# Two attentions of a float32 encoder trunk: other orders in their first stretches and around the start of their output projections

## The chip, the cores and the metric

One Trainium2 chip, one of its cores. The metric is device time in microseconds (us) of one launch of the whole program; lower is better. Engines: PE is TensorE, ACT ScalarE, DVE VectorE, POOL GpSimd, SP SyncE (it issues most DMAs). Each runs its own instruction stream in order and waits on semaphores.

## The reference, cut to what matters

Two layers over x of 1024 tokens by 1024 features, float32:

```python
for i in range(DEPTH):                    # DEPTH = 2
    hn = rmsnorm(x, norm_mix[i])
    if i == 0:  x = x + windowed_gqa_attention(hn, w_qkv, w_o, sink)    # 16 heads of 64, 4 KV groups, |t-s| <= 128
    else:       x = x + differential_attention(hn, w_qkv, w_o, lam, subln_g, lambda_init)   # 8 heads, two maps each
    x = x + hierarchical_moe(rmsnorm(x, norm_ffn[i]), ...)              # 32 experts, top-1 group, top-2 experts
return rmsnorm(x, final_norm)
```

Both attentions project `hn @ w_qkv`, form softmax(q k^T + bias) v by blocks of 128 queries, and multiply the heads' outputs by `w_o`. In the second, each head's output also goes through an RMSNorm of its own before `w_o`.

## The kernel before, in words

The program is a row of blocks: attention 0 (`windowed_attention`), routing and experts of layer 0, attention 1 (`differential_attention`), routing and experts of layer 1, final norm. All engines meet at the end of each. Every large product is made in three float32r passes: each operand is split into a high part (a cast on ScalarE) and a low part (a subtraction on VectorE or GpSimd), and `three_passes` (lines 365 to 367) multiplies hi by hi, lo by hi and hi by lo. One slice k of a product is a contraction over 128.

**First stretch of an attention.** `Norm` walks over the 8 token tiles (128 tokens each). For tile tt ScalarE squares and sums (line 302) and takes the root (305), VectorE makes the normalised rows (335), TensorE turns them in 8 transposes (358) into two PSUM banks, ScalarE copies them out as the high part (314) and VectorE subtracts (276) to get the low part. Both loops run the copy and the subtraction of tile tt - 2 in step tt. In steps 5, 6 and 7 ("meanwhile") ScalarE and VectorE also split three column blocks j of the first head's weights (407, 413). In attention 0 x comes by four DMAs of two tiles each; in attention 1 two gathered expert rows per tile are added to x first (line 234, twice per tile). TensorE turns tiles 0 to 5, then does projection piece 0 (24 matmuls of 512 columns), turns tiles 6 and 7, then does pieces 1 to 5. A piece (j, n) needs all low parts of tile half n and those of weight block j.

**Attention blocks.** Attention 0 goes over 4 groups, attention 1 over 8 heads, each with 8 query blocks i: scores on TensorE, bias and maximum on VectorE (698; 1413), exponentials on ScalarE, normalising or mixing on VectorE (713; 1430), turns on TensorE (814; 1548), copies on ScalarE (608; 1359), the product with v on TensorE. The groups and heads but the last run in a loop, and the last is written out apart.

**Output projection.** `OutProjection` reads `w_o` by 8 row blocks k through three staging buffers (SyncE loads block k + 3 once k's low part is done). In the last group or head ScalarE casts block i in query block i (474) and GpSimd subtracts (478). After all query blocks, tile tt of the heads' outputs is split (650 and 674; in attention 1 first scaled, 1486, and turned, 1597, then 1377 and 1493), TensorE multiplies it with all 8 weight blocks (48 matmuls, 6 per k), and VectorE adds x and clears the banks (501). In attention 1 the roots of all 8 tiles' sums (1371) are taken after the last head.

Of the kernel before, what the change touches and what calls it, by code (L numbers as in the profile page):

```python
# [21 lines left out]
P = 128  # L22
T = 1024
D = 1024
NT = T // P
# [159 lines left out]
class Loaded(Resident):  # L185


    def __init__(self, t, x_rows):
        self.t, self.x_rows = t, x_rows
        self.loaded = [t.sem(f"x_loaded_{i}") for i in range(NT // 2)]  # L190

    def load(self, sp):
        for i, loaded in enumerate(self.loaded):
            sp.dma_start(self.t.x[:, 2 * i:2 * i + 2, :], self.x_rows[2 * i * P:2 * (i + 1) * P, :]
                         .rearrange("(a p) n -> p a n", p=P)).then_inc(loaded, 16)

    def complete(self, eng, tt):
        eng.wait_ge(self.loaded[tt // 2], 16)
# [43 lines left out]
class Norm:  # L242
# [3 lines left out]
    def __init__(self, t, name, number, sb, banks, source, tiles_T=0, rows_dram=None, bufs=2):  # L246
# [47 lines left out]

    def scalar(self, act, meanwhile=()):

        for tt in range(NT + 2):
# [9 lines left out]
            if 0 <= tt - NT // 2 - 1 < len(meanwhile):  # L307
                meanwhile[tt - NT // 2 - 1]()
            if tt >= 2:
                done = tt - 2  # L310
# [3 lines left out]
                act.copy(self.tile_T(done) if self.tiles_T else self.hi[:, :, done * P:(done + 1) * P],  # L314
                         self.turned_tile(done)).then_inc(self.copied, 1)

    def vector(self, dve, meanwhile=(), second=None):
# [3 lines left out]
        for tt in range(NT):  # L321
# [22 lines left out]
            if not self.tiles_T and tt >= 2:  # L344
                self.low_part(dve, tt - 2)
            if 0 < tt - NT // 2 <= len(meanwhile):
                meanwhile[tt - NT // 2 - 1]()
        if not self.tiles_T:
            self.low_part(dve, NT - 2)
            self.low_part(dve, NT - 1)  # L350
# [19 lines left out]
class Projections:  # L370
# [45 lines left out]
    def tensor(self, pe, out, step, o, first, ks=range(KD)):  # L416


        j, n = self.order[o]
        if first and o == 0:  # L420
            for tt in range(NT - 2):
                self.norm.turn(pe, tt)
        if first and o == 1:
# [14 lines left out]
class OutProjection:  # L438
# [42 lines left out]
    def tensor(self, pe, tt):  # L481
        pe.wait_ge(self.o_lo_done, 2 * tt + 2)
        for k in range(KD):
# [10 lines left out]
        last.then_inc(self.done, 1)  # L494
# [10 lines left out]
def windowed_attention(t, gain, w_qkv, w_o, sink, x_rows, args):  # L505
# [10 lines left out]
    with ExitStack() as ctx:  # L516
# [44 lines left out]
        with nc.Block() as block:  # L561
            @block.sync
            def _(sp):
                t.gain.load(sp, gain)
                norm.source.load(sp)
                sp.dma_start(sinks[:, :], sink.broadcast_to((P, NQ))).then_inc(sink_loaded, 16)

                projections.load(sp, 0)
# [20 lines left out]
            def _(act):  # L589
# [1512 lines left out]
```

## Time and profile before

| | us |
|---|---|
| median of 3 runs (range) | 2495.68 (2493.53 to 2496.23) |
| the profiled execution's own time | 2497.94 |
| its span | 2496.3 |
| TensorE busy, share of span | 2307.5, 92% |
| VectorE busy | 1870.3, 75% |
| ScalarE busy | 1554.3, 62% |
| GpSimd busy | 264.7, 11% |
| attention 0 / attention 1, from the span's start | about 2 to 443 / 1074 to 1820 |

The profile page gives the span in 40 slices; in the slices of the two attentions TensorE is at 9 tenths except at their starts, and in the expert stages DMA is at 9 tenths. Busy shares are averages over the stages. An instruction's idle time stands in square brackets with what released it; matmul ends are modelled, and start to start is the better measure.

### The profile page before, as it was taken

Reading aid. Unit: us, or ns where it says so; the run is one execution under the profiler, and the core shown is the slowest. Engines: PE = TensorE matmul, PEld = TensorE weight load, DVE = VectorE, ACT = ScalarE, POOL = GpSimd, SP = SyncE. Lnnn points to the kernel's source line nnn. Section 1 sums busy time; section 2 is a strip of 40 time slices with the busy share of each in tenths; the row PEclk is TensorE's granted clock in tenths of the full one; section 3 lists DMA queues with packets and bytes.
Section 4 is the critical chain, followed back from the end, with each engine's and each line's share of the span. In section 5 each row is a group of like instructions: output and inputs, shape, how many; then the busy total and the mean of one; then the engine's idle time right before and its main releaser. Section 6 shows DMA issues by size and latency. Waiting matters only on the chain. (4 is left out here: it accounts for less than half of the span.)

```text
span 2496.3 us, 34756 instructions
## 1 busy us (share of the span) xinstructions
PE 2307.5 (92%) x11480; PEld 1748.9 (70%) x11480; DVE 1870.3 (75%) x2487; ACT 1554.3 (62%) x2037; POOL 264.7 (11%) x256
## 2 busy tenths in 40 slices
PE   7999989699999999939999999998969999999991
PEld 6667768577777777628888888886856777777671
DVE  6776672799898988867666667655279989888895
ACT  5565450577877777746555666554147777777772
POOL 0000020022111111130000000002001111121113
PEclk9999999799999999969999999999989999999996
DMA  3022021599999999852000000002149999999995
GB/s 127 26 64 95 26 76 45 194 378 393 401 394 402 395 402 393 342 193 88 11 26 25 25 25 25 3 31 67 45 177 363 398 400 398 401 395 398 394 371 214
DMA packets 132051, 538.62 MB, mean 216 GB/s; under 512 B 25776, under 2 KB 54576, under 8 KB 82832
## 3 DMA queue, kind: packets, MB, share of 16 engines
q1 hardware_dynamic: 113040, 470.67, 49.3%
q0 software_dynamic: 18944, 67.12, 7.7%
q8 instruction: 35, 0.57, 0.1%
q14 instruction: 32, 0.26, 0.0%
HBM read 487.54 MB, written 50.20 MB: 215 GB/s over the span
## 5 line engine op out<-in xcount | busy, mean ns | idle before, releaser
L1710 DVE TENSOR_TENSOR m_lo_gate<-m_raw_gate,m_hi_gate 128x2048 fp32r<-128x2048 f32 x132 | 301.4, 2291 | 75.2 <-ACT m_hi_gate L1705 73.0
L1710 DVE TENSOR_TENSOR m_lo_up<-shared,m_hi_up 128x2048 fp32r<-128x2048 f32 x128 | 292.4, 2287 | 13.4 <-ACT m_hi_up L1705 12.0
L1710 DVE TENSOR_TENSOR m_lo_down<-m_raw_down,m_hi_down 128x2048 fp32r<-128x2048 f32 x124 | 282.2, 2284 | 16.8 <-ACT m_hi_down L1705 16.7
L1705 ACT CAST m_hi_gate<-m_raw_gate 128x2048 fp32r<-128x2048 f32 x132 | 250.7, 1908 | 67.4 <-DMA m_raw_gate<-in_moe_w_gate_dram 63.4
L1705 ACT CAST m_hi_down<-m_raw_down 128x2048 fp32r<-128x2048 f32 x124 | 236.3, 1908 | 87.6 <-DMA m_raw_down<-in_moe_w_down_dram 85.9
L1705 ACT CAST m_hi_up<-shared 128x2048 fp32r<-128x2048 f32 x128 | 244.6, 1912 | 38.9 <-DMA shared<-in_moe_w_up_dram 38.3
L1841 PE MATMUL m_G<-m_hi_gate,m_x_hi 128*96 128x512 f32 x512 | 205.6, 402 | 3.8 <-DVE m_x_lo L1963 3.3
L1841 PE MATMUL m_U<-m_hi_up,m_x_hi 128*96 128x512 f32 x512 | 204.8, 400 | 0.0
L1843 PE MATMUL m_G<-m_lo_gate,m_x_hi 128*96 128x512 f32 x512 | 204.0, 398 | 0.0
L1842 PE MATMUL m_G<-m_hi_gate,m_x_lo 128*96 128x512 f32 x512 | 203.0, 396 | 0.0
L1843 PE MATMUL m_U<-m_lo_up,m_x_hi 128*96 128x512 f32 x512 | 202.0, 395 | 0.0
L1842 PE MATMUL m_U<-m_hi_up,m_x_lo 128*96 128x512 f32 x512 | 200.9, 392 | 0.0
L1841 PE MATMUL m_Y<-m_hi_down,m_h_hi 128*96 128x512 f32 x496 | 198.0, 399 | 0.0
L1842 PE MATMUL m_Y<-m_hi_down,m_h_lo 128*96 128x512 f32 x496 | 195.4, 394 | 0.0
L1843 PE MATMUL m_Y<-m_lo_down,m_h_hi 128*96 128x512 f32 x496 | 194.0, 391 | 0.0
L1413 DVE CUSTOM_DVE_ANT_0 shared<-a_S,a_bias 128x1024 f32<-128x1024 f32 x128 | 151.6, 1222 | 22.2 <-PE a_S L1531 11.9
L1314 ACT ACTIVATE shared<-shared 128x1024 f32<-128x1024 f32 x128 | 146.1, 1144 | 29.2 <-DVE shared L1418 27.6
L365 PE MATMUL a_S<-a1n_hi,a_w_hi 128*128 128x512 f32 x384 | 156.2, 407 | 0.0
L367 PE MATMUL a_S<-a1n_lo,a_w_hi 128*128 128x512 f32 x384 | 152.8, 398 | 0.0
L366 PE MATMUL a_S<-a1n_hi,a_w_lo 128*128 128x512 f32 x384 | 152.7, 398 | 0.0
L1714 POOL DMA_INDIRECT m_xg<-hn_rows,m_pick x56 | 103.8, 1853 | 415.1 <-PE m_XT L1854 415.1
L1560 PEld LDWEIGHTS a_TO<-a_v_rows,a_mix 128*128 128x128 f32 x1024 | 123.3, 192 | 11.7 <-issue 6.6
(377 smaller groups left out, 4916.5 us busy)
## 6 DMA issues: line engine op xcount, KB each, us to landing
m_raw_gate<-in_moe_w_gate_dram SPq DMA_DIRECT2D x128, 1024.0 KB, 13.2
shared<-in_moe_w_up_dram SPq DMA_DIRECT2D x128, 1024.0 KB, 12.9
m_raw_down<-in_moe_w_down_dram SPq DMA_DIRECT2D x124, 1024.0 KB, 12.2
out_rows<-m_y POOLq DMA_DIRECT2D x64, 384.0 KB, 7.3
a1n_rows<-in_diff_w_qkv_dram SPq DMA_DIRECT2D x21, 512.0 KB, 5.6
out_rows<-gain_b SPq DMA_DIRECT2D x1, 8064.0 KB, 37.1
x_res<-in_x_dram SPq DMA_DIRECT2D x4, 1024.0 KB, 9.7
a0n_rows<-in_swa_w_o_dram SPq DMA_DIRECT2D x8, 512.0 KB, 3.3
```

What stands on the lines that cost most here:

```text
L365: pe.matmul(out, left[0], right[0], start=first, stop=False)
L366: pe.matmul(out, left[1], right[0], start=False, stop=False)
L367: return pe.matmul(out, left[0], right[1], start=False, stop=last)
L1314: last = act.activation(row, row, ACT.Exp, bias=neg2[:, i % 2, c:c + 1], accum_out=sum2[:, i % 2, c:c + 1])
L1413: dve.tensor_tensor_reduce(probs[:, i % 2, c, :].rearrange("p (a b) -> p a b", a=2), S[:, 2 * c:2 * c + 2, :], bias[:, at:at + T].rearrang ...
L1560: last = pe.matmul(O[:, i % 2, 0:VD], mixT[:, i % 2, k * P:(k + 1) * P], v_rows[:, k, :], start=(k == 0), stop=(k == KD - 1))
L1705: act.copy(self.hi[w][:, cut], self.raw[w][:, cut]).then_inc(self.hi_done[w], 1)
L1710: eng.tensor_tensor(self.lo[w][:, cut], self.raw[w][:, cut], self.hi[w][:, cut].bitcast(F32), ALU.subtract)\
L1714: pool.indirect_dma_start(out=self.xg[:, :], out_offset=None, in_=self.hn_rows, in_offset=bass.IndirectOffsetOnAxis(rows, 0)).then_inc(sel ...
L1841: pe.matmul(out[n], l_hi[:, rows], r_hi[:, cols], start=(k == 0), stop=False)
L1842: pe.matmul(out[n], l_lo[:, rows], r_hi[:, cols], start=False, stop=False)
L1843: last = pe.matmul(out[n], l_hi[:, rows], r_lo[:, cols], start=False, stop=(k == K - 1))
```

## The change

It edits both attentions only. In words:

- `Loaded`: x comes by 8 DMAs of one tile. In attention 0 SyncE issues tile 0, the gain row, tiles 1 to 5, the first weights, tiles 6 and 7, the sinks. Before: gain, x, sinks, weights.
- `Norm.table`: one small root is ScalarE's first instruction in both attentions.
- `Norm` has a `lag`: 2 as before in attention 0; in attention 1 it is 1, so copy and subtraction of tile tt - 1 stand in step tt, and the weight blocks are split in steps 4, 5 and 7.
- Attention 1's first projections: TensorE turns tiles 0 to 4 ahead, tile 5 between slices 3 and 4 of piece 0, tiles 6 and 7 before slices 2 and 6 of piece 1. The bias' last step on VectorE (line 1391) moves behind the norm.
- Attention 0's output projection: weight blocks 0, 1, 2 are cast in query blocks 2, 3, 5, the rest after block 7; output tiles 0 and 1 are cast in blocks 4 and 6; TensorE does slice 0 of tile 0 in block 6, slices 1 and 2 in block 7, then tile 1's slices 0 to 2, then slices 3 to 7 of both tiles in turns.
- Attention 1's output projection: weight blocks (0,1), 2, (3,4), 5, 6, 7 are cast in query blocks 0 to 5; tile 0's root is taken in block 6; its scaling, turn and split run in and behind block 7, into banks 2 and 3 of the scores; TensorE turns tile 1 between slices 4 and 5 of tile 0.
- The last group's and head's bias scaling and padding steps on VectorE go.

```diff
             def _(sp):
+                norm.source.load(sp, range(1))
                 t.gain.load(sp, gain)
-                norm.source.load(sp)
+                norm.source.load(sp, range(1, NT - 2))
+                projections.load(sp, 0)
+                norm.source.load(sp, range(NT - 2, NT))
                 sp.dma_start(sinks[:, :], sink.broadcast_to((P, NQ))).then_inc(sink_loaded, 16)
-
-                projections.load(sp, 0)
...
+    def table(self, act):
+        act.activation(self.first_root[:, :], self.t.eps_col[:, :], ACT.Sqrt, bias=self.t.zero_col[:, :])
...
+        between = {(0, 4): NT - 3, (1, 2): NT - 2, (1, 6): NT - 1} if first and early else {}
         for k in ks:
+            if (o, k) in between:
+                self.norm.turn(pe, between[o, k])
...
+                        if last_group and i in (2, 3, 5):
+                            out_proj.high_weights(act, (2, 3, 5).index(i))
+                        if last_group and i in (4, 6):
+                            output_parts(i // 2 - 2)
...
+                        if last_group and i == 7:
+                            out_proj.tensor(pe, 0, range(1, 2))
                         pe.wait_ge(probs_ready, n + 1)
...
+                        if last_group and i >= 6:
+                            out_proj.tensor(pe, 0, (range(0, 1), range(2, 3))[i - 6])
...
-                for tt in range(NT):
+                out_proj.tensor(pe, 1, range(0, 3))
+                for k in range(3, KD):
+                    for tt in range(2):
+                        out_proj.tensor(pe, tt, range(k, k + 1))
+                for tt in range(2, NT):
                     out_proj.tensor(pe, tt)
...
-                        if last_head:
-                            out_proj.high_weights(act, i)
+                        if last_head and i < NT - 2:
+                            for k in ((0, 1), (2,), (3, 4), (5,), (6,), (7,))[i]:
+                                out_proj.high_weights(act, k)
+                        if last_head and i == NT - 2:
+                            act.wait_ge(o_squared, NT * h + 3)
+                            root(slice(0, 1))
...
+                        if last_head and i == NT - 1:
+                            turn_o(0)
...
+                out_proj.tensor(pe, 0, range(0, 5))
+                turn_o(1)
+                out_proj.tensor(pe, 0, range(5, KD))
```

## Rows read from the trace of the kernel before

**Rows 1.** Timeline of ScalarE, attention 0's first stretch: start, us, what, [idle before <-releaser].

```profile
8.76 1.15 ACT L302 ACTIVATE a0n_rows<-x_res,zero_col 128x1024 f32<-128x1024 f32 x1 [5.53 <-DMA x_res<-in_x_dram]
...
10.02 1.28 ACT L305 ACT_TABLE_LOAD   x1
...
22.77 1.04 ACT L407 CAST a_w_hi<-shared 128x1024 fp32r<-128x1024 f32 x1 [0.29 <-DMA shared<-in_swa_w_qkv_dram]
```

**Rows 2.** DMA issues by line, first 60 us: KB of each, median us to landing.

```profile
x_res<-in_x_dram SPq DMA_DIRECT2D x4, 1024.0 KB, 9.7
...
gain_b<-in_norm_mix_dram SPq DMA_DIRECT2D x1, 512.0 KB, 4.3
```

**Rows 3.** Timeline of TensorE, attention 0's first projection matmul.

```profile
27.73 0.77 PE L365 MATMUL a_S<-a0n_hi,a_w_hi 128*128 128x512 f32 x1
```

**Rows 4.** Timeline of VectorE, attention 1's first stretch.

```profile
1084.31 2.15 DVE L1391 SCALAR_TENSOR_TENSOR a_bias<-a_bias 128x1920 f32<-128x1920 f32 x1
...
1108.11 1.28 DVE L335 SCALAR_TENSOR_TENSOR a1n_rows<-x_res,a1n_rstd,gain_b 128x1024 f32<-128x1024 f32 x1
...
1116.75 2.67 DVE L234 SCALAR_TENSOR_TENSOR x_res<-shared,choice_weight,x_res 128x1024 f32<-128x1024 f32 x2
...
1126.79 2.54 DVE L276 TENSOR_TENSOR a1n_lo<-a_TO,a1n_hi 128x1024 fp32r<-128x1024 f32 x2
...
1133.18 1.39 DVE L1447 SCALAR_TENSOR_TENSOR a_q_parts<-a_S,a_q_parts 64x512 fp32r<-64x512 f32 x2 [3.02 <-DMA x_rows<-x_res]
```

**Rows 5.** Timeline of TensorE, attention 1's first two projection pieces.

```profile
1117.44 0.77 PE L365 MATMUL a_S<-a1n_hi,a_w_hi 128*128 128x512 f32 x1
...
1126.77 0.48 PE L365 MATMUL a_S<-a1n_hi,a_w_hi 128*128 128x512 f32 x1
```

**Rows 6.** Windows: busy (x instructions) of each engine, TensorE's granted clock, DMA, GB/s.

```profile
1115.00:1120.00 5.00, 4.15 (x14) 3.70 (x15) 4.79 (x6) 2.10 (x3) 0.00 (x0) 0.50 0.00 0
```

**Rows 7.** DMA issues in 1091.2 to 1094: third slice of attention 1's first weights.

```profile
a_mix<-in_diff_w_qkv_dram SPq DMA_DIRECT2D x1, 512.0 KB, 18.3
```

**Rows 8.** Timeline of TensorE, attention 0, group 2: turns of its second and eighth block.

```profile
233.48 1.03 PE L814 MATMUL a_TO<-ident,shared 128*128 128x128 f32 x8
...
266.73 1.04 PE L814 MATMUL a_TO<-ident,shared 128*128 128x128 f32 x8
```

**Rows 9.** The same of group 3, and the output projection's first matmul.

```profile
312.17 1.03 PE L814 MATMUL a_TO<-ident,shared 128*128 128x128 f32 x8
...
349.49 1.04 PE L814 MATMUL a_TO<-ident,shared 128*128 128x128 f32 x8
...
353.15 0.50 PE L365 MATMUL a_S<-a0n_hi,a_w_hi 128*128 128x512 f32 x1 [0.29 <-DVE a_w_lo L674]
```

**Rows 10.** Timeline of TensorE: the last matmul of attention 0's output projection.

```profile
442.62 0.40 PE L367 MATMUL a_S<-a0n_lo,a_w_hi 128*128 128x512 f32 x1
```

**Rows 11.** Timeline of VectorE, attention 0's last group and output projection.

```profile
320.95 1.56 DVE L702 TENSOR_TENSOR a_top<-a_top,a_sink 128x4 f32<-128x4 f32 x1
...
364.75 1.29 DVE L501 TENSOR_TENSOR x_res<-a_S,a0n_rows 128x512 f32<-128x512 f32 x2 [6.68 <-PE a_S L367]
365.96 1.28 DVE L674 TENSOR_TENSOR a_w_lo<-x_res,a_w_hi 128x512 fp32r<-128x512 f32 x2
```

**Rows 12.** Timeline of GpSimd over the same stretch.

```profile
320.13 2.36 POOL L478 TENSOR_TENSOR a0n_lo<-a0n_rows,a0n_hi 128x1024 fp32r<-128x1024 f32 x1 [4.16 <-ACT a0n_hi L474]
```

**Rows 13.** Timeline of VectorE, attention 1's last head and output projection.

```profile
1692.67 1.33 DVE L1418 TENSOR_SCALAR shared<-shared 128x2 f32<-128x2 f32 x1
...
1737.29 1.29 DVE L501 TENSOR_TENSOR x_res<-a_S,a1n_rows 128x512 f32<-128x512 f32 x2 [11.59 <-PE a_S L367]
```

**Rows 14.** Timeline of TensorE, attention 1's last turn and its output projection's start.

```profile
1711.49 1.04 PE L1548 MATMUL a_TO<-ident,a_mix 128*128 128x128 f32 x8
...
1719.48 1.97 PE L1597 MATMUL a_TO<-ident,x_res 128*128 128x128 f32 x8 [4.54 <-DVE x_res L1486]
...
1723.84 0.78 PE L365 MATMUL a_S<-a1n_hi,a_w_hi 128*128 128x512 f32 x1
```

More of the change, by code:

```diff
@@ L306, in scalar @@
                                scale=1.0 / D).then_inc(self.rms_ready, 1)
[L307 to L310, printed above, removed]
+            if self.lag == 2 and tt in self.meanwhile_at:
+                meanwhile[self.meanwhile_at.index(tt)]()
+            if tt >= self.lag:
+                done = tt - self.lag
                 act.wait_ge(self.turned, done + 1)
@@ L343, in vector @@
                    .then_inc(self.hn_ready, 1)
[L344 to L347, printed above, removed]
+            if not self.tiles_T and tt >= self.lag:
+                self.low_part(dve, tt - self.lag)
+            if tt in self.meanwhile_at:
+                meanwhile[self.meanwhile_at.index(tt)]()
         if not self.tiles_T:
-            self.low_part(dve, NT - 2)
-            self.low_part(dve, NT - 1)
+            for tt in range(NT - self.lag, NT):
+                self.low_part(dve, tt)
     def turn(self, pe, tt):
@@ L419, in tensor @@
         j, n = self.order[o]
+        early = self.norm.lag == 1
         if first and o == 0:
-            for tt in range(NT - 2):
+            for tt in range(NT - 3 if early else NT - 2):
                 self.norm.turn(pe, tt)
-        if first and o == 1:
+        if first and o == 1 and not early:
             self.norm.turn(pe, NT - 2)
@@ L493, in tensor @@
                                     (self.w_hi[:, k, cols], self.w_lo[:, k, cols]), k == 0, k == KD - 1)
-        last.then_inc(self.done, 1)
+        if KD - 1 in ks:
+            last.then_inc(self.done, 1)
     def vector(self, dve, tt):
@@ L589, in _ @@
             def _(act):
+                norm.table(act)
                 norm.scalar(act, [lambda j=j: projections.high_part(act, 0, j) for j in range(3)])
@@ L1301, in _ @@
             def _(act):
+                norm.table(act)
                 act.wait_ge(iota_done, 1)
@@ L1347, in head, with root @@
                             exponentials(0)
+                    def root(tiles):
+                        act.activation(o_rms[:, tiles, :], o_ss[:, tiles, :], ACT.Sqrt, bias=sub_eps[:, :], scale=1.0 / VD)\
+                           .then_inc(rms_out, 1)
                     for i in range(NT):
@@ L1366, in head, with output_parts @@
                     act.wait_ge(o_squared, NT * h + NT)
-                with act.Fori(0, HEADS - 1) as h:
-                    head(h, False)
-                head(HEADS - 1, True)
-                act.activation(o_rms[:, :, :], o_ss[:, :, :], ACT.Sqrt, bias=sub_eps[:, :], scale=1.0 / VD).then_inc(rms_out, 1)
-                for tt in range(NT):
+                    if last_head:
+                        root(slice(1, NT))
+                def output_parts(tt):
                     for b in range(2):
```

103 lines of the change are left out of this document (62 added, 41 removed).

## The prediction

> **What bounds the kernel now.** I read the page first for where TensorE is not busy, then the timelines of all engines over the four places that the diff touches, then the DMA issues there. The expert stages hang on their weight transfers, and nothing of them is edited. All engines meet at the end of each block, so a microsecond saved inside an attention shifts all behind it. TensorE is full in the attentions but at four places.
>
> At attention 0's start TensorE multiplies first at 27.73 [rows 3]. ScalarE starts when the first two tiles of x are there, at 8.76, loads a second function table at 10.02, and at 22.77 waits for the first weights [rows 1]. These arrive behind the gain row and four 1 MB pieces of x [rows 2].
>
> At attention 1's start VectorE has no pause from 1084.31 to 1129.33 [rows 4]; it is the bound. TensorE's first piece starts at 1117.44, the second at 1126.77 [rows 5].
>
> In attention 0's last group the eighth block's turn starts 37.32 after the second's (312.17 to 349.49) [rows 9]; in group 2 it is 33.25 [rows 8]. The 4.07 more come with GpSimd's weight subtractions. One runs from 320.13 to 322.49 [rows 12], and VectorE's 128x4 operation, begun at 320.95, takes 1.56 and ends with it [rows 11]. VectorE sets that block's pace.
>
> At attention 1's end the last turn is at 1711.49. TensorE then idles 4.54 before it turns the first output tile at 1719.48, and multiplies only from 1723.84 [rows 14].
>
> **The change, part by part.** One three-pass matmul of 512 columns costs (442.62 - 353.15) / 383 = 0.2336 start to start [rows 9, 10].
>
> *Attention 0's start.* Tile 0 lands before the gain, about as the first 512 KB does now, in 4.3 [rows 2] after its issue near 2: at 6.3, so 2.5 before 8.76. The second table load, 1.28 [rows 1], also leaves the path, so ScalarE would reach the weights some 3.5 earlier. They are late next: 3.5 MB stand before them where 4.5 MB do now, and 1 MB takes 8.76 - 6.3 = 2.5. ScalarE thus waits about 1 there and all behind it is 2.5 earlier. Tiles 6 and 7 now queue behind the weights; at 2.5 per MB they land at about 21.3 and 22.5, and ScalarE wants them at 22.1 and 25.4. Four more issues and the weights moved past the sinks on SyncE are covered by the transfers. If the weights were not last the gain is 3.5, if their many small rows rather than bytes set their end, 1. I take **2.5** (1 to 3.5).
>
> *Attention 1's start.* The bias step, 2.15 at 1084.31 [rows 4], moves behind the norm, where VectorE has been waiting 3.02 for the x stores before 1133.18 [rows 4]; without that cover it would cost 2.15. The lag of 1 puts one low part (2.54 / 2) earlier into the row. So the rows of tile 4, at 1108.11 now, start at about 1107.2 and end at 1108.5; low part 3 and weight low part 0 end at 1110.8. There TensorE can start piece 0, 6.6 before 1117.44. Going on with 2.67 for a tile's two adds [rows 4], tile 6's rows end at 1121.2. Its turn (1.1), slices 2 to 5 (12 x 0.2336 = 2.8), the turn of tile 7 (1.1), ScalarE's copy (1.2) and the low part (1.2) end at 1128.7. Piece 2 needs that. Now it starts 24 x 0.2336 = 5.6 after 1126.77, at 1132.4. That is 3.7 earlier. The x stores are as late as before; behind 1133.2 VectorE has 1.4 + 2.8 + 1.4 + 1.2 + 2.8 of parts to make, ready about when TensorE has done piece 4 at 1145.6. The first weights' third slice took 18.3 to land [rows 7], just before ScalarE splits them at 1109.4; ScalarE now wants them at 1106.2. They are asked for 2 earlier and their low part has 1 in hand, so I charge 0.1. The early root is worth nothing here, since VectorE's first adds hide the table load. I take **3.6** (1.5 to 4.2).
>
> *Attention 0's end.* Three weight splits instead of six fall between the second and the eighth turn; VectorE also does one output split (1.28 [rows 11]) there and ScalarE two. Each hold costs VectorE some 1.4. I take back half of the 4.07: 2.0. TensorE's 18 matmuls of tile 0 (4.2) fill about 1.0 of waiting in block 6, 0.4 in block 7 and the 0.29 before 353.15 [rows 9]: 1.7. Against this stands a new wait. Slices 3 to 7 alternate, so tile 0 ends only 6 matmuls, 1.4, before tile 1. Tile 2 needs its o parts: after tile 0's end (the add starts at 364.75) the low part is done at 365.96 + 1.28 = 367.24 [rows 11], 2.9 after the last matmul. Now a whole tile covers that; then 1.5 is bare, and all six later tiles are queued behind. The five late weight splits need 2.4 each on GpSimd and TensorE uses a slice in 12 x 0.2336 = 2.8, with 4.2 of other matmuls ahead of them; they hide. 2.0 + 1.7 - 1.5 = **2.2** (0 to 4.5: from no pace regained to all of it). The padding steps that go lay under matmuls: 0.
>
> *Attention 1's end.* From the last turn at 1711.49: turn 1.05, the first output turn 1.05, the product with v 1.95, some 0.7 until the low part is there, 48 matmuls 11.2 and a turn 1.05 give 1728.5 for tile 0's end, where 1737.1 was (the add starts at 1737.29 [rows 13]): 8.6. This counts on TensorE staying at its higher clock; it now stands idle first and pays some 2 at the lower. The root in block 6 puts a table load (1.28) and 0.35 in place of a cast of 0.93 ahead of copies that TensorE waits for: -0.7. Now the holds. A weight split holds VectorE's small step at 1692.67 for 1.2 [rows 13]. Two casts in a row in blocks 0 and 2 make GpSimd run twice, 2.36 [rows 12] longer, and the third cast comes earlier, onto VectorE's mixing step: 2.4 + 1.3 = 3.7 more. 8.6 - 0.7 - 3.7 = **4.2** (0.5 to 7.9).
>
> **Sum.** 2.5 + 3.6 + 2.2 + 4.2 = 12.5. The profiled execution took 2497.94 and would take 2485.4. It lies 2.26 above the median of the runs, so I forecast 2483.2. Differences within 0.2%, 5 us, can hardly be told from no change.
>
> **The rivals.** *Nothing is held longer* (10%): GpSimd's pairs fall beside VectorE's bank reads, and attention 0's pace comes back whole. 3.7 and 2.0 more: 2477.5. For it speaks that the first of eight splits in attention 1 held nobody; against it, six of the others did.
>
> *VectorE is held whole* (17%): both operations of a pair, and splits that land on the normalising steps of attention 0, stop VectorE to GpSimd's end. Attention 1's end gives 0.5, attention 0's end 0, and 2489.1 results. The place is blocks 0 to 3 of the last head. The Trainium skill, SBUF — State Buffer, section "SBUF: two separate sides", says that VectorE and GpSimd share a port pair as an exclusive lock held for a whole instruction, the loser fully blocked. By that rule this rival is the nearer one; the trace agrees as far as 1.56 for a 128x4 step goes [rows 11], but shows no pair.
>
> *The transfers set the starts* (8%), so that the reordering does not do what it is for: weights in attention 0 land 0.5 earlier, in attention 1 no earlier, and its start gives 1.5. 12.5 - 2.0 - 2.1 = 8.4: 2487.3. The 18.3 [rows 7] speaks for it.
>
> *TensorE's clock* (4%), the other side: slower. In 1115 to 1120 the granted clock was 0.50, 1.2 GHz [rows 6], after a stretch of lone turns. The interleaved pieces now pause for turns. If the clock stayed at 0.50 through all 144 matmuls of the first head, each would cost up to 0.2336 more, 33.6 less the 2 paid today: 2514. It decides from 75 such matmuls on (17.5 / 0.2336). Against it: the pauses are under 1 us. The Trainium skill, TensorE: Matmul & The Clock Gate, section "HAM oscillation — how this bites in real kernels", describes products with waits between them falling back to half clock again and again; no row of this trace shows it for pauses this short.
>
> **How the numbers follow.** The forecast has 61%, with 2480 to 2487 as its own range; the others as given. 2476 to 2491 takes in no longer holds, whole holds and late transfers, and leaves out the clock and the outer ends. Faster: 61 + 10 + 11 of the 17 + 7 of the 8 = 0.89; same: the rest of these two, 0.07; slower: 0.04.
>
> **What would show it.** Attention 0: first matmul at about 25.2; ScalarE's wait for the weights about 1. Attention 1: a first matmul 26.5 after the point at which VectorE now starts its bias step (1084.31 to 1110.8), piece 2 some 3.7 earlier against the block's start. Attention 0's last group: turns two to eight in about 37 with 2.8 of output matmuls among them, and a gap of 1.5 before output tile 2. Attention 1's end: no idle above 1 between the last product with v and the output projection, and the higher clock from its first matmuls on; VectorE's steps of over 3 in blocks 1 to 3. I would be wrong if a pair of casts delays ScalarE's copies so that TensorE stalls on these instead, or if the weights' landing follows their count of rows and not what is queued ahead.

## The result and the profile after

The changed kernel took 2479.38 us (median of four runs, 2475.54 to 2481.22) against 2494.61 for the kernel before beside it: a ratio of 0.9938, 95% interval 0.9925 to 0.995. A second set of five runs on another occasion gave 0.9945 (0.9932 to 0.9959). The change saves some 14 to 15 us; the prediction had 12.5. The profiled execution of the changed kernel took 2477.91, which is 20.0 below the profiled one of before; the ledger below shows that 15.7 of this lie inside the attentions and the rest mostly in the expert stages.

The first stretch of attention 0 on ScalarE, to be held against [rows 1]:

```profile
5.80 1.15 ACT L306 ACTIVATE a0n_rows<-x_res,zero_col 128x1024 f32<-128x1024 f32 x1 [2.26 <-DMA x_res<-in_x_dram]
...
8.92 1.15 ACT L306 ACTIVATE a0n_rows<-x_res,zero_col 128x1024 f32<-128x1024 f32 x1 [1.55 <-DMA x_res<-in_x_dram]
...
19.46 1.05 ACT L413 CAST a_w_hi<-shared 128x1024 fp32r<-128x1024 f32 x1 [0.19 <-DMA shared<-in_swa_w_qkv_dram]
```

TensorE's first projection matmul, to be held against [rows 3]:

```profile
24.42 0.77 PE L371 MATMUL a_S<-a0n_hi,a_w_hi 128*128 128x512 f32 x1
```

ScalarE's first square stands at 5.80 and not at 8.76, and the first weight split at 19.46 and not at 22.77: 3.3 are saved, and TensorE multiplies at 24.42. The second square waits 1.55 for its tile. That hole is wide enough for a table load of 1.28, which comes into play in the first experiment on this place.

TensorE in attention 0's last group and behind it, to be held against [rows 9, 10]:

```profile
307.66 1.04 PE L838 MATMUL a_TO<-ident,shared 128*128 128x128 f32 x8
...
344.44 1.04 PE L838 MATMUL a_TO<-ident,shared 128*128 128x128 f32 x8
...
368.04 0.50 PE L371 MATMUL a_S<-a0n_hi,a_w_hi 128*128 128x512 f32 x1 [1.25 <-DVE a_w_lo L694]
...
435.11 0.40 PE L373 MATMUL a_S<-a0n_lo,a_w_hi 128*128 128x512 f32 x1
437.23 1.94 PE L1044 MATMUL m0r_T<-ident,x_res 128*128 128x128 f32 x16 [1.72 <-PEq L572]
```

The second block's turn is 4.51 earlier than in [rows 9], the last matmul of the output projection 7.51 earlier than in [rows 10]. The stall in front of output tile 2 is there, 1.25 long.

VectorE at attention 1's start and TensorE's pieces, to be held against [rows 4, 5]:

```profile
1070.33 1.28 DVE L233 SCALAR_TENSOR_TENSOR x_res<-shared,choice_weight,x_res 128x1024 f32<-128x1024 f32 x1 [16.18 <-DMA shared<-out_rows,choice_slot]
1072.77 1.28 DVE L233 SCALAR_TENSOR_TENSOR x_res<-shared,choice_weight,x_res 128x1024 f32<-128x1024 f32 x1 [1.16 <-DMA shared<-out_rows,choice_slot]
...
1074.68 2.66 DVE L233 SCALAR_TENSOR_TENSOR x_res<-shared,choice_weight,x_res 128x1024 f32<-128x1024 f32 x2
```

```profile
1100.72 0.77 PE L371 MATMUL a_S<-a1n_hi,a_w_hi 128*128 128x512 f32 x1 [0.39 <-DVE a_w_lo L419]
...
1118.20 0.50 PE L371 MATMUL a_S<-a1n_hi,a_w_hi 128*128 128x512 f32 x1 [0.97 <-DVE a1n_lo L277]
```

The row that began with the bias step at 1084.31 begins at 1074.68 with the adds. The first matmul comes 26.0 behind it (33.1 before), piece 2, which starts at 1118.20, 43.5 behind it (48.1 before).

VectorE and GpSimd in attention 1's last head, to be held against [rows 13]; the TENSOR_SCALAR takes 0.17 when it is let alone, the 128x1 step 0.22 and the reciprocal 0.15:

```profile
1666.50 1.99 DVE L1467 TENSOR_SCALAR shared<-shared 128x2 f32<-128x2 f32 x1
...
1668.66 0.15 DVE L1473 RECIPROCAL shared<-shared 128x2 f32<-128x2 f32 x1
1668.84 1.97 DVE L1474 SCALAR_TENSOR_TENSOR a_ratio<-shared,a_lam_neg 128x1 f32<-128x1 f32 x1
...
1674.75 2.28 DVE L1467 TENSOR_SCALAR shared<-shared 128x2 f32<-128x2 f32 x1
```

```profile
1663.00 7.80 POOL L488 TENSOR_TENSOR a1n_lo<-a1n_rows,a1n_hi 128x1024 fp32r<-128x1024 f32 x3 [568.93 <-ACT a1n_hi L484]
1672.28 4.72 POOL L488 TENSOR_TENSOR a1n_lo<-a1n_rows,a1n_hi 128x1024 fp32r<-128x1024 f32 x2 [1.49 <-ACT a1n_hi L484]
```

Read the ends: VectorE's steps end at 1668.49, 1670.81 and 1677.03, GpSimd's second, third and fifth subtraction at 1668.5, 1670.8 and 1677.0. The small step stands until GpSimd is done. Not every step does: the reciprocal at 1668.66 also reads and writes SBUF, starts inside the third subtraction and takes its usual 0.15. Six holds sum to 9.1 us. In the kernel before five sum to 5.8, and the longest of them is on the mixing step, which takes 1.28 when it is let alone:

```profile
1681.70 3.34 DVE L1430 SCALAR_TENSOR_TENSOR a_mix<-shared,a_ratio 128x1024 f32<-128x1024 f32 x1
```

TensorE at attention 1's end, to be held against [rows 14], and then the windows over it (us, busy and instructions of each engine, granted clock, DMA share, GB/s):

```profile
1696.54 1.06 PE L1601 MATMUL a_TO<-ident,a_mix 128*128 128x128 f32 x8 [1.82 <-issue]
1699.18 3.75 PE L1615 MATMUL a_TO<-a_v_rows,a_mix 128*128 128x128 f32 x16 [1.57 <-ACT a_mix L1399]
1702.72 1.92 PE L1601 MATMUL a_TO<-ident,a_mix 128*128 128x128 f32 x8
1704.43 1.31 PE L1647 MATMUL a_S<-ident,x_res 128*128 128x128 f32 x8
...
1707.52 0.51 PE L371 MATMUL a_S<-a1n_hi,a_w_hi 128*128 128x512 f32 x1
```

```profile
1698.00:1700.00 2.00, 0.82 (x4) 0.85 (x5) 1.97 (x3) 1.90 (x6) 0.00 (x0) 0.54 0.00 0
1700.00:1702.00 2.00, 2.00 (x11) 2.00 (x11) 0.09 (x1) 0.00 (x0) 0.00 (x0) 0.50 0.03 8
...
1704.00:1706.00 2.00, 2.00 (x15) 2.00 (x15) 0.00 (x0) 1.71 (x4) 0.00 (x0) 0.76 0.00 0
1706.00:1708.00 2.00, 2.00 (x16) 1.76 (x15) 1.76 (x3) 1.81 (x8) 0.00 (x0) 1.00 0.00 0
```

The idle 4.54 of [rows 14] is gone, as forecast. But between 1698 and 1705 the granted clock is at 0.50 and a product with v takes 3.75. Ahead of it TensorE stood idle for 1.82 and 1.57. In the kernel before the second of these waits is 0.90:

```profile
1709.63 2.02 PE L1560 MATMUL a_TO<-a_v_rows,a_mix 128*128 128x128 f32 x16 [0.90 <-ACT a_mix L1359]
```

**A ledger of stretches.** Total times scatter by several us from one execution to the next, stretches inside an attention by less (E0 by 0.05, the other three by 2 to 3 over all profiles, for reasons given below). So I use four stretches, each read from TensorE's and VectorE's timelines: S0, from the span's start to the second block's turn of attention 0's last group; E0, from there to the first turn of the routing; S1, from attention 1's first add to the first biased scores; E1, from the first turn of the last head to the first turn of the next routing. In us:

| kernel | S0 | E0 | S1 | E1 |
|---|---|---|---|---|
| before | 312.2 | 132.6 | 71.3 | 147.4 |
| changed | 307.7 | 129.6 | 66.0 | 144.4 |
| difference | 4.5 | 3.0 | 5.3 | 2.9 |

These make 15.7 of the 20.0 between the two profiles. From the routing's first turn to attention 1's first add the one profile has 634.5 and the other 633.1, behind the second routing's first turn 674.1 and 671.3. The change edits nothing there, and over all profiles of this study the first of these stretches lies anywhere from 632.7 to 636.0.

### The profile page after: what moved, and what is told of

Same layout as the page of the kernel before. It is cut to its first block and busy times, and to the rows that moved or that the text cites. A ratio compares the mean times of both kernels' runs of the same rounds, so it can differ in the third digit from the quotient of the medians.

```text
span 2476.2 us, 34758 instructions
## 1 busy us (share of the span) xinstructions
PE 2301.7 (93%) x11480; PEld 1746.2 (71%) x11480; DVE 1856.6 (75%) x2476; ACT 1551.1 (63%) x2039; POOL 277.7 (11%) x256
## 5 line engine op out<-in xcount | busy, mean ns | idle before, releaser
L1761 ACT CAST m_hi_gate<-m_raw_gate 128x2048 fp32r<-128x2048 f32 x132 | 247.9, 1908 | 33.9 <-DMA m_raw_gate<-in_moe_w_gate_dram 32.0
L1770 POOL DMA_INDIRECT m_xg<-hn_rows,m_pick x56 | 127.9, 2283 | 393.4 <-PE m_XT L1910 393.4
```

The lines of the kernel that those rows point to most:

```text
L1761: act.copy(self.hi[w][:, cut], self.raw[w][:, cut]).then_inc(self.hi_done[w], 1)
L1770: pool.indirect_dma_start(out=self.xg[:, :], out_offset=None, in_=self.hn_rows, in_offset=bass.IndirectOffsetOnAxis(rows, 0)).then_inc(sel ...
```

## The experiments

**One part alone, added to the kernel before.** Each kernel has one of the four parts and nothing of the others. The core of each edit:

```diff
 start0_only
-            sp.dma_start(self.t.x[:, 2 * i:2 * i + 2, :], ...
+            sp.dma_start(self.t.x[:, tt, :], ...
...
+                norm.source.load(sp, range(1, NT - 2))
+                projections.load(sp, 0)
+                norm.source.load(sp, range(NT - 2, NT))
...
+                norm.table(act)
 start1_only
+        norm = Norm(t, "a1n", 2, ..., lag=1)
...
+                distances()
 end0_only
+                        if last_group and i in (2, 3, 5):
+                            out_proj.high_weights(act, (2, 3, 5).index(i))
...
+                        if last_group and i >= 6:
+                            out_proj.tensor(pe, 0, (range(0, 1), range(2, 3))[i - 6])
 end1_only
+                            for k in ((0, 1), (2,), (3, 4), (5,), (6,), (7,))[i]:
+                                out_proj.high_weights(act, k)
...
+                        if last_head and i == NT - 1:
+                            turn_o(0)
```

> The kernel before with the start of attention 0 alone changed (x by tiles, the first weights ahead of the last two tiles, the early root). Theory A, read from the profile after: the first projection matmul comes 3.3 us earlier (24.4 instead of 27.73), and TensorE's clock rises within the first few matmuls after it and not near 31, which gives about 1.2 more; the second block's turn in the last group stands at 307.7 instead of 312.17, and the whole kernel gains 4.5. Theory B, the prediction's term: 2.5 in all, the rest of the 4.5 came from elsewhere in the changed kernel. Rival C: the clock's part is chance and is not seen again, so 3.3.

> The kernel before with the start of attention 1 alone changed (lag of one tile, projection slices between the turns, the bias step behind the norm, the early root). Theory A, from the profile after: from the first add of the block to the first biased scores it takes 66.0 us instead of 71.3 (1079.25 to 1150.55 before), 5.3 gained. Theory B, the prediction's term: 3.6. Rival C: 0.7 of the 5.3 is only an earlier landing of the rows that the block gathers, which this edit does not touch, so 4.6 of the edit.

> The kernel before with the end of attention 0 alone changed. Theory A, from the profile after: 3.0 us gained between the second block's turn of the last group and the first turn of the routing (132.6 before, 129.6 after), with a wait of about 1.25 before output tile 2. Theory B, the prediction's term: 2.2. Rival C: the end gains only with the earlier start of the block, because where GpSimd's subtractions fall against VectorE's steps is set by when the weights land; then the gain is off from 3.0 by more than 1 either way.

> The kernel before with the end of attention 1 alone changed. Theory A, from the profile after: 2.9 us gained from the last head's first turn to the first turn of the next routing (147.4 before, 144.4 after), with seven intervals of turns of 42.3 instead of 36.6 and the output tile's end 8.6 nearer to the last of these turns. Theory B, the prediction's term: 4.2, and the last 1.3 were lost to a placing of GpSimd's work that will not repeat. The whole kernel gains as much.

| kernel | ratio to before, 95% interval | S0 | E0 | S1 | E1 |
|---|---|---|---|---|---|
| start0_only | 0.9979 (0.9970 to 0.9988) | **308.2** | 132.6 | 70.7 | 149.1 |
| start1_only | 0.9976 (0.9965 to 0.9987) | 312.5 | 132.6 | **66.2** | 149.1 |
| end0_only | 0.9987 (0.9978 to 0.9997) | 312.7 | **129.5** | 70.1 | 146.2 |
| end1_only | 0.9973 (0.9962 to 0.9984) | 311.1 | 132.6 | 70.3 | **144.3** |

Each part is faster by itself, and in each the stretch that it edits (bold) is within 0.6 of the changed kernel's. E0 gains 3.0 whether attention 0 began early or late, so the third expectation's rival C is out. S0 gains 4.0 and not 4.5, since the clock rose later than in the profile after. S1 gains 5.1 against the one profile of before, but 4.4 against the mean of the four kernels with the old start (70.6), so the second expectation's rival C is the nearest. The four ratios would add up to 21 us, more than the 14 to 15 of the whole change, but each carries 2 to 3 us of uncertainty, and the stretches add up without such a surplus.

E1 is not as stable as I had thought: kernels whose end is that of before have 146.2 to 149.1. What differs is TensorE's clock. In start0_only and start1_only the product of the last block but one takes 3.75 and in before 2.02. A gain read from one pair of profiles there is uncertain by 2 to 3. In end1_only this product took 3.75 too.

The kernels from here on, but for the last two, were executed once each (2492.49, 2496.33, 2490.32, 2471.74, 2475.64 and 2473.78, in the order below). I compare their stretches and not these totals.

**Two single edits in one kernel, at two far places.**

```diff
 attention 0: the order of the loads, without the early root
+                norm.source.load(sp, range(1, NT - 2))
+                projections.load(sp, 0)
+                norm.source.load(sp, range(NT - 2, NT))
 attention 1: the bias step behind the norm, with the old lag
                 norm.vector(dve, [lambda j=j: ...], parameters)
+                distances()
```

> The kernel before with two single edits at two far places: in attention 0 the order of the loads and x by tiles, without the early root; in attention 1 the bias step behind the norm, without the lag. Theory A: in attention 0 the weights' landing is what the order moves, and ScalarE reaches them some 1.3 us later than with the early root (20.6 instead of 19.3), so the first projection matmul comes at 25.8: the order gives 2.2 of the 3.5, the early root the rest. In attention 1 the bias step gives its own 2.15 of the 4.5, the lag the other 2.3. Rival: the early root gives nothing in attention 0, the first matmul stands at 24.5; and the bias step gives less than 1.5, because its 2.15 only go from one place of VectorE's row to the other.

ScalarE's timeline of this kernel at attention 0's start:

```profile
5.63 1.15 ACT L306 ACTIVATE a0n_rows<-x_res,zero_col 128x1024 f32<-128x1024 f32 x1 [2.40 <-DMA x_res<-in_x_dram]
...
6.89 1.28 ACT L309 ACT_TABLE_LOAD   x1
...
9.01 1.15 ACT L306 ACTIVATE a0n_rows<-x_res,zero_col 128x1024 f32<-128x1024 f32 x1 [0.54 <-DMA x_res<-in_x_dram]
...
19.57 1.05 ACT L413 CAST a_w_hi<-shared 128x1024 fp32r<-128x1024 f32 x1 [0.21 <-DMA shared<-in_swa_w_qkv_dram]
```

The rival holds. The second table load is back on ScalarE, but it runs in the hole in which ScalarE waits for the second tile of x (0.54 are left of that wait). The first projection matmul is at 24.53 and S0 is 308.3, as with the early root. The order and size of the loads are the whole gain; the early root is worth nothing.

S1 was 71.3: nothing gained. VectorE waited for gathered rows, and so the bias step was tried once more alone, and the lag alone beside it:

> The kernel before with the bias step behind the norm in attention 1, and nothing else. In the run of order and bias, 71.3 us lay between the first add and the first biased scores of attention 1, as before the change, and VectorE waited 0.95, 0.92 and 1.86 for gathered rows that the step of 2.15 had covered. Theory A: the landing of the gathered rows differs from run to run, this was one late landing, and alone the step is worth about 2 (68.5 us). Theory B: without the lag VectorE always catches up with the gather, and moving the step is worth under 0.7 (70 us or more).

> The kernel before with the lag of one tile and the projection slices between the turns in attention 1; the bias step stays where it was. With both, the stretch from the first add to the first biased scores took 66.0 to 66.8 us, and 70.1 to 71.3 without either. Theory A: the lag is worth 2.3 (68.3 us). Theory B: it is worth nearly all of the 4.2 (66.5 us), since the projection's start hangs on the last tiles and not on the first.

The edits are, in the first, the move of the bias step as above, and in the second:

```diff
-        norm = Norm(t, "a1n", 2, sb, TO, Combined(...))
+        norm = Norm(t, "a1n", 2, sb, TO, Combined(...), lag=1)
```

VectorE's adds of gathered rows in the kernel with the bias step moved alone:

```profile
1089.71 1.28 DVE L234 SCALAR_TENSOR_TENSOR x_res<-a_v_rows,choice_weight,x_res 128x1024 f32<-128x1024 f32 x1 [0.60 <-DMA a_v_rows<-out_rows,choice_slot]
...
1093.77 1.28 DVE L234 SCALAR_TENSOR_TENSOR x_res<-shared,choice_weight,x_res 128x1024 f32<-128x1024 f32 x1 [1.38 <-DMA shared<-out_rows,choice_slot]
1096.46 1.28 DVE L234 SCALAR_TENSOR_TENSOR x_res<-shared,choice_weight,x_res 128x1024 f32<-128x1024 f32 x1 [1.41 <-DMA shared<-out_rows,choice_slot]
```

S1 is 71.1 with the bias step alone (theory B) and 68.2 with the lag alone (theory A). The step of 2.15 that goes from VectorE's row comes back as waits of 0.60, 1.38 and 1.41 for the gather. The lag is worth 2.4. With both, S1 was 65.9 to 66.8 in six profiles and 68.2 in a seventh, where VectorE waited 1.80 and 0.84 for these rows. So the bias step's 2 are real with the lag, where the gather lands in time, and were not seen without it.

The wait for the x stores, which ends at the first q parts, splits S1 in two. These are its rows in the kernel with the lag alone and in the changed one:

```profile
1132.52 1.39 DVE L1459 SCALAR_TENSOR_TENSOR a_q_parts<-a_S,a_q_parts 64x512 fp32r<-64x512 f32 x2 [4.17 <-DMA x_rows<-x_res]
```

```profile
1123.13 1.39 DVE L1496 SCALAR_TENSOR_TENSOR a_q_parts<-a_S,a_q_parts 64x512 fp32r<-64x512 f32 x2 [2.54 <-DMA x_rows<-x_res]
```

From there to the first biased scores it is 13.2 to 13.4 in all eight profiles with the lag and 17.1 to 17.4 in all six without: 4 less. From the first add to there it is 52.8 to 53.9 in the four kernels with the old start, 55.0 with the lag alone, and 52.6 to 53.6 with both (55.1 in the seventh profile). So the lag puts the stores off, presumably by the low part of 1.2 that it moves ahead of the last adds, and the move of the bias step takes this back. Whether without the lag the bias step would show where the gather lands in time, these runs don't settle: both profiles have late rows.

**GpSimd's subtractions made small.** Changed kernel, with 8 of 1,024 columns (the low parts of the output weights are left out but for these):

```diff
-        pool.tensor_tensor(self.w_lo[:, k, :], self.staged(k), self.w_hi[:, k, :].bitcast(F32), ALU.subtract)\
+        pool.tensor_tensor(self.w_lo[:, k, 0:8], self.staged(k)[:, 0:8], self.w_hi[:, k, 0:8].bitcast(F32), ALU.subtract)\
```

> The changed kernel with GpSimd's weight subtractions cut to 8 of 1,024 columns in both attentions (the low parts of the output weights are left out but for those). Theory A: these subtractions hold VectorE's small step in the last head of attention 1 for 9.1 us in sum (1.8, 1.8, 2.1 and three times 1.15); without them the eight turns there take some 34 to 36 us and not 42.3. In attention 0's last group next to nothing is held since the change, so its part from the second turn to the routing stays at 129.6 within 0.5. Rival B: the pace of the last head is set by ScalarE's casts in front of its copies, and the turns stay at 41 or more. Rival C: attention 0's end gets faster as well, by more than 1.

The eight turns of the last head take 33.7 and not 42.3, E1 is 134.9. E0 stays at 129.5 to a tenth. Of these 8.6 the clock is 1.7: here the product of the last block but one takes 2.02 and not 3.75. Against the other profile of the changed kernel (below), where it takes 2.02 too and the turns 40.6, the subtractions cost 6.9 at attention 1's end. At attention 0's they cost nothing. Rivals B and C are out.

**One cast for each block; and tile 0 ahead in attention 0.**

```diff
-                            for k in ((0, 1), (2,), (3, 4), (5,), (6,), (7,))[i]:
-                                out_proj.high_weights(act, k)
+                            out_proj.high_weights(act, i)
...
                             output_parts(0)
+                            for k in (6, 7):
+                                out_proj.high_weights(act, k)
...
-                for k in range(3, KD):
+                for k in (3, 4):
                     for tt in range(2):
                         out_proj.tensor(pe, tt, range(k, k + 1))
+                for tt in range(2):
+                    out_proj.tensor(pe, tt, range(5, KD))
```

> The changed kernel with two edits. In attention 1's last head one weight cast for each of blocks 0 to 5 and not two in blocks 0 and 2, the last two behind the first output tile's parts. In attention 0 the slices 5 to 7 of output tile 0 ahead of those of tile 1. Theory A: the pairs cost 9.1 minus 6 x 1.15 = 2.2 us in the last head's turns. In attention 0 the wait of 1.25 before output tile 2 goes, and the end of attention 0 takes 128.3 and not 129.6. Rival: the holds are as long with single casts (the first, in block 0, holds as two did), under 0.7 gained in attention 1; and in attention 0 the weights' low parts are late for tile 0's slices 5 to 7, so that TensorE waits there instead.

The turns take 39.0, 3.3 less (with a product of 3.75 in both), since the holds are those of the kernel before, 5.8 in sum; I had expected 2.2. E0 is 128.0, 1.5 less, and the stall in front of output tile 2 is gone. Both rivals are out.

**The cast between the two exponentials.** As the kernel above in attention 1, and the changed one in attention 0, but:

```diff
                         for c in range(2):
+                            if c == 1 and weights is not None:
+                                out_proj.high_weights(act, weights)
                             row = probs[:, i % 2, c, :]
```

> The changed kernel with one weight cast for each of blocks 0 to 5 of attention 1's last head, as in the run of single casts, but put between the two exponentials of a block and not behind them. GpSimd then starts 1.15 us earlier. Theory A: VectorE is held only where one of its operations between two SBUF operands meets GpSimd, and its 2.3 us of work that reads the scores' banks is not; GpSimd's 2.4 then fall beside just this, the hold of 1.15 for each block shrinks to under 0.3, and the turns take 42.3 - 2.2 - 5 = 35 us. Rival B: the hold is the same wherever GpSimd starts, since each of its operations costs VectorE about 1.2; no better than single casts.

VectorE's two held steps and its first pass over the scores' banks in the block behind them, and under them GpSimd's third subtraction in this kernel:

```profile
1666.39 2.21 DVE L1468 TENSOR_SCALAR shared<-shared 128x2 f32<-128x2 f32 x1
...
1672.87 0.43 DVE L1468 TENSOR_SCALAR shared<-shared 128x2 f32<-128x2 f32 x1
...
1675.42 1.23 DVE L1463 CUSTOM_DVE_ANT_0 shared<-a_S,a_bias 128x1024 f32<-128x1024 f32 x1 [0.22 <-DVE a_mix L1480]
```

```profile
1675.59 2.40 POOL L488 TENSOR_TENSOR a1n_lo<-a1n_rows,a1n_hi 128x1024 fp32r<-128x1024 f32 x1 [2.31 <-ACT a1n_hi L484]
```

The turns take 33.9. Of the holds 2.3 are left, nearly all of it in one step, and no other 128x2 step is over 0.2. GpSimd works as long as before (2.40 for one), only at another moment: from 1675.59 to 1677.99 it runs beside VectorE's two passes over the scores' banks (from 1675.42 on, 1.23 and 1.22 as ever) and nobody waits. Rival B is out: it matters what VectorE does while GpSimd runs. Theory A's number came out (35 expected), but its condition, any operation between two SBUF operands, is too wide: the reciprocal shown above is one, and was not held. Of the 5.1 between 39.0 and 33.9 the clock is 1.7 (the product takes 2.02 again), the moved cast 3.4.

**All of it mended, and the changed kernel again beside it.** The two edits above, and the first output tile's root behind ScalarE's copies:

```diff
-                        if last_head and i == NT - 2:
-                            act.wait_ge(o_squared, NT * h + 3)
-                            root(slice(0, 1))
...
                             act.copy(mixT[:, i % 2, ...], TB[:, b, :]).then_inc(mixT_ready, 1)
+                        if last_head and i == NT - 2:
+                            act.wait_ge(o_squared, NT * h + 3)
+                            root(slice(0, 1))
```

> The changed kernel with single casts between the two exponentials, the slices 5 to 7 of attention 0's output tile 0 first, and the first output tile's root in attention 1 behind ScalarE's copies of its block and not ahead of them. Expected from the single runs: the last head's turns take 33.9 us and not 42.3, the end of attention 0 takes 128.0 to 128.3 and not 129.6; the late root gives up to 0.7 more in the last two turns. In all 9 to 11 us below the changed kernel: 2469 to 2471. Rival: the late root makes TensorE wait for the scaled tile before the first output turn, which costs what the copies gain, so 2470 to 2472; or holds saved in the last head are spent again by the last two subtractions beside the scaling steps, 2474.

> The changed kernel once more, unedited, on the same chip as the mended one, for the comparison with it and for what differs between two executions of one program. Theory: the stretches inside the attentions come out within 1 us of the first profile (129.6 from the second block's turn to the routing, 66.0 to 66.8 at attention 1's start, 144.4 at its end), and what differs between the profiles lies in the expert stages and in how soon TensorE's clock rises. Rival: the first profile was a lucky one, and the changed kernel's gain is the 12.5 of the prediction and not the 15 to 16 of the first comparison.

The mended kernel took 2469.93 (0.9904 of before, 0.9889 to 0.992), the changed one 2479.95 on the same chip: 10.0 less. Its E0 is 128.0, its E1 134.5. With the clock high in both, the two edited stretches make 8.7 of the 10.0, 1.5 and 7.2. The late root cuts TensorE's wait of 1.57 to 0.39 and puts one of 0.61 in front of the first output turn, as its rival said, so it is worth 0.5 in E1.

The changed kernel again has S0 308.4, E0 129.5, S1 68.2 and E1 141.7. So the theory, all stretches within 1 us, failed in S1 (the gather) and in E1, and chance is not only in the expert stages. Its rival stays open: the second comparison gives 13.7, with 12.5 inside its interval of 10 to 17. E1 is 2.7 under that of the first profile. TensorE in that stretch of this execution:

```profile
1699.82 1.06 PE L1601 MATMUL a_TO<-ident,a_mix 128*128 128x128 f32 x8 [1.82 <-issue]
1702.46 2.02 PE L1615 MATMUL a_TO<-a_v_rows,a_mix 128*128 128x128 f32 x16 [1.57 <-ACT a_mix L1399]
1704.32 1.04 PE L1601 MATMUL a_TO<-ident,a_mix 128*128 128x128 f32 x8
...
1706.06 1.95 PE L1615 MATMUL a_TO<-a_v_rows,a_mix 128*128 128x128 f32 x16
```

The same two products that took 3.75 and 1.95 in the first profile take 2.02 and 1.95 here, behind the same two idle times of 1.82 and 1.57; the granted clock stays at 1.00. The same program falls to the lower clock at this place in one execution and not in the next.

## Why the prediction was right

The time, the direction and most of the mechanism came out as forecast; each of the four parts gains. The median of 2479.38 lies within the stated 2476 to 2491 and just under the forecast's own range, 2480 to 2487: three of the four terms were too small. By means over all profiles with and without a part:

| part | predicted | measured | from |
|---|---|---|---|
| start of attention 0 | 2.5 | 3.7 | S0: six without, 312.1; eight with, 308.4 |
| end of attention 0 | 2.2 | 3.0 | E0: 132.6 and 129.5, each within 0.05 |
| start of attention 1 | 3.6 | 4.0 | S1: four without, 70.6; seven with, 66.6 |
| end of attention 1 | 4.2 | 4.1 | E1: seven without, 147.6; three with, 143.5 |
| sum | 12.5 | 14.8 | ratios: 15.5 and 13.7 |

**Attention 0's start.** The step "ScalarE thus waits about 1 there" was off: the wait is 0.19. ScalarE is ready for the weights 3.2 earlier (19.27 for 22.48), 3.5 predicted, and their last slice lands 3.3 earlier (19.44 for 22.75), 2.5 predicted. The landing is the term that was too small. The weights do end ScalarE's wait: in all 14 profiles the cast starts within 0.03 of the landing of the last weight slice, after waits of 0.06 to 0.67. With the old order the longest stands in start1_only:

```profile
23.24 1.05 ACT L414 CAST a_w_hi<-shared 128x1024 fp32r<-128x1024 f32 x1 [0.66 <-DMA shared<-in_swa_w_qkv_dram]
```

Of the 3.3, the transfers ahead of the weights give 2.5 (the last of x ahead of them lands at 14.03 for 16.57), as predicted for 1 MB less. The other 0.8 is that the weights land 5.4 behind it and not 6.2. The sinks no longer go between, which the prediction counted as covered, and the third slice is issued at 6.93 and not at 13.59, which it left out; no run tells the two apart. The first matmul comes 3.5 earlier (28.0 to 24.5 in the mean). That this is the 3.5 of the prediction's start without bound weights is luck: that sum had the table load in it, which gives nothing, and left out the weights, which set the moment. The remaining spread, 311.1 to 312.7 without and 307.7 to 309.2 with the part, is mostly the clock's (below).

**Attention 0's end.** The stall of 1.5 is there with 1.25, and it is shown to be the order of the slices. Pace and filled waits, 3.7 predicted, make about 4.3. The turns of the second to the eighth block take 36.8 with 2.8 of output matmuls among them, where 37.3 [rows 9] held none; the prediction said "about 37". All these 2.8 fall between the turns of the seventh and eighth block and lengthen that interval by 2.0, from 5.24 to 7.28. The five intervals before it hold none and shrink from 32.1 to 29.5; in group 2 they take 27.9. So the pace came back by 2.6, where half of the 4.07 was predicted, and the waits filled come to 1.7 as what is left of 4.3. The pace's 0.6 and the stall's 0.2 are what the term lacked. GpSimd holds nobody there any more, and with its subtractions cut to 8 columns the intervals stay as they are, so the 1.6 that are still missing against group 2 are not its doing; what they are is open.

**Attention 1's start.** Predicted: the first matmul 26.5 behind the row's start, piece 2 some 3.7 earlier against it. Measured: 26.0 and 4.6. The x stores still end the wait before the q parts, 2.54 long now, and in the mean as late as before (53.3 behind the first add, with the part and without), as said; the gain of 4 lies behind them. The step that I left out is the gather: I moved 2.15 of cover away from it and named no price. It cost 3.4 of waits where the step was moved alone, and 2.6 and 1.2 in two of the seven profiles with the whole part.

**Attention 1's end.** That 4.1 was measured for 4.2 is partly luck. The stretch from the last turn to the next routing takes 110.7 before and 101.2 in the second profile of the changed kernel, where the clock stays high: 9.6 of structure, 8.6 predicted. Holds 3.7 longer: 3.3 (9.1 less 5.8). Root 0.7: the wait behind it is 1.57 and not 0.90, 0.7. That makes 5.6, and this profile has 5.6 less than before. "This counts on TensorE staying at its higher clock" held in it alone. In the other two profiles with the new end the lower clock cost 2.6 to 2.7, of which 1.7 ahead of the last turn, and left 2.9 and 3.1. The mean of three profiles, against seven of which two had a slow product of their own, happens to meet the term.

The Trainium skill, SBUF — State Buffer, section "SBUF: two separate sides", says that the pair shared by VectorE and GpSimd is an exclusive lock held for a whole instruction, and names a VectorE operation with two SBUF inputs or in a two-port mode as what competes for it. The traces agree as far as they go: held steps stand until GpSimd's end (1.99 for 0.17), and the pass that reads its scores from the banks takes 1.22 beside GpSimd and without it. The held TENSOR_SCALAR has one input; whether it ran in a two-port mode no run shows. The rival built on this, both operations of each pair held whole, was wrong. The first operation of each pair ran mainly beside VectorE's passes over the banks and held nobody. The second ones held it for 1.82 and 2.11, and the single one of block 1 for 1.75; the other three holds begin in the middle of GpSimd's run and last 1.1 each, and at attention 0's end nothing was held. For the same reason the steps of over 3 that the forecast named as its sign did not come, the longest being 2.28. The sum of 3.3 for 3.7 was right, its parts were not.

Of the other rivals, that nothing is held longer is refuted by the 9.1. That transfers set the starts is true of attention 0 as a mechanism, since the weights' landing ends ScalarE's wait, and refuted in its size: it had them 0.5 earlier, and they came 3.3 earlier. In attention 1 the transfer that mattered is another one, the gather. The lower clock through attention 1's first head did not come: 4 to 11 matmuls of it are slow, with and without the pauses for turns.

## What to carry to other kernels

What a subtraction on GpSimd costs VectorE depends on when it runs: moving one cast by one instruction, so that GpSimd's subtraction, as long as ever, falls beside VectorE's reads of the PSUM banks, gave 3.4 in the last head's turns (39.0 to 33.9, less 1.7 of the clock), about as much as one of the four parts of the change. Before taking work away ahead of a transfer, ask how long the transfer was covered by it. When single edits are worth a few microseconds of 2,500, compare stretches between fixed points of the timeline over several executions; much of the total's scatter comes from stages that nobody edited. Where the clock can fall inside a stretch, sort its profiles by that first.

## What the runs showed of the hardware

- How soon TensorE speeds up differs between executions of one stretch. Behind the first projection matmul of attention 0 the matmuls are 0.43 apart and then 0.23. In six profiles with the old start the slow ones number 9, 9, 8, 7, 4 and 2, in eight with the new one 2 to 9, and S0 goes with that number. Each costs 0.2. It is the clock: the spacing changes where the trace's clock record goes to 1.00, at 31.67 in the kernel before. In twelve of the 14 traces this record begins only there, and a window ahead of it reads 1.00 for want of an entry. In the other two (order_and_bias, bias_alone) it begins earlier and reads 0.50. These are windows over such slow matmuls, in the kernel before and in order_and_bias:

```profile
28.00:30.00 2.00, 2.00 (x6) 1.53 (x5) 2.00 (x3) 1.97 (x5) 0.00 (x0) 1.00 0.00 0
```

```profile
24.00:26.00 2.00, 2.00 (x9) 1.71 (x8) 1.90 (x2) 1.99 (x3) 0.00 (x0) 0.50 0.00 0
```

Early in a program the spacing is the safer reading.
- The same at attention 1's end: idle times of 1.82 and 1.57 were followed by a granted clock of 0.50 for some 7 us in one execution and by none in another.
- A gather of one program can land 1.9 us later in another execution (11.16 behind the first add and not 9.25): GpSimd issued it 1.0 later, and it was 0.9 longer under way.
- VectorE's TENSOR_SCALAR, TENSOR_TENSOR and SCALAR_TENSOR_TENSOR with all operands in SBUF were held by a GpSimd subtraction that was running when they began (0.17 alone and 1.99 held; 0.16 and 1.56 [rows 11]; 1.28 and 3.34). A RECIPROCAL in SBUF took its 0.15 beside one.
